# Rounded products in the input and value projections of block 2

## What is computed

```
n1 = _rmsnorm(h, norm1_w)
proj = n1 @ w_in
q, k, v, fg, u = jnp.split(proj, [512, 1024, 1536, 1544], axis=-1)
q, k = rmsnorm of q and k by head;  cum_logf = cumsum(log_sigmoid(fg + b_fgate))
a_out = softmax(q k^T / 8 + cum_logf[t] - cum_logf[s], causal) v
p_out = (trailing means of u, minus u) @ w_pool * pool_scale
h = h + concat(a_out, p_out) @ w_out
h = h + (silu(n2 @ w_gate) * (n2 @ w_up)) @ w_down
```

## Time and profile before

| | |
|---|---|
| median of 3 runs | 2333.66 us (2331.21 to 2335.54) |
| profiled execution | 2334.32 us, span 2332.6 us |
| TensorE matmul busy | 1959.3 us, 84% |
| VectorE busy | 1395.7 us, 60% |
| ScalarE busy | 1074.3 us, 46% |
| GpSimd busy | 582.4 us, 25% |
| mean granted TensorE clock | 0.905 |

### The profile page before, as it was taken

One profiled execution on the slowest core, in us unless ns is written; L12 is line 12 of the kernel. 1 busy time (PEld: TensorE's weight loads), 2 busy tenths in 40 slices (PEclk: granted clock), 3 DMA queues, 4 the chain that ended last, 5 costly groups with the idle time before them and its releaser, 6 DMA issues.

```text
span 2332.6 us, 41079 instructions
## 1 busy us (share of the span) xinstructions
PE 1959.3 (84%) x16124; PEld 1344.2 (58%) x16124; DVE 1395.7 (60%) x3264; ACT 1074.3 (46%) x2533; POOL 582.4 (25%) x541
## 2 busy tenths in 40 slices
PE   5888897988888779877855988889888885999999
PEld 4767785655545546545522623356665553667887
DVE  6654678686776676656577576666555533123554
ACT  3334545455555652224344758634454213343443
POOL 0000003332223343334344234433333330000000
PEclk8999998998888889998966996689999997999999
DMA  9932449998889999999999999999999994313555
GB/s 343 340 123 73 162 136 386 390 385 340 322 326 409 402 418 418 417 419 418 417 418 414 410 396 402 382 418 417 418 417 418 418 418 173 137 46 127 183 180 169
DMA packets 140497, 758.52 MB, mean 325 GB/s; under 512 B 16224, under 2 KB 22496, under 8 KB 74384
## 3 DMA queue, kind: packets, MB, share of 16 engines
q0 software_dynamic: 74784, 543.30, 57.1%
q1 hardware_dynamic: 60864, 208.23, 24.0%
q10 hardware_dynamic: 4656, 4.36, 0.6%
HBM read 751.60 MB, written 4.23 MB: 324 GB/s over the span
## 4 chain that ended last, share of the span: by engine, by line
PE 44%; DMA 30%; ACT 10%; DVE 10%; issue 4%; POOL 2%; ACTq 0%; SPq 0%; DVEq 0%
DMA arena<-experts,eidx 27%; PE psum L1324 7%; PE psum L842 4%; DVE arena L2475 4%; PE psum L843 4%; PE psum L844 4%; PE psum L1172 4%; DMA ring<-w_stream 2%; POOL arena L2452 2%; PE psum L1448 2%; PE psum L1621 2%; PE psum L1498 2%; DVE ring_low L2495 2%; ACT arena L2096 1%; PE psum L1197 1%
## 5 line engine op out<-in xcount | busy, mean ns | idle before, releaser
L2475 DVE CUSTOM_DVE_ANT_0 arena<-arena 128x1024 f32<-128x1024 f32 (+3 forms) x592 | 691.6, 1182 | 398.5 <-DMA arena<-experts,eidx 372.1
L2452 POOL DMA_INDIRECT arena<-experts,eidx x512 | 573.6, 1120 | 1203.8 <-PE psum L1324 925.6
L1324 PE MATMUL psum<-arena,sq 32*32 32x512 f32 x8192 | 372.2, 710 | 278.4 <-ACT sq L2104 265.6
L2090 ACT ACTIVATE arena<-arena 128x2 f32<-128x2 f32 x256 | 51.8, 202 | 585.5 <-DVE arena L2475 582.7
L1324 PEld LDWEIGHTS psum<-arena,sq 32*32 32x32 f32 x8192 | 84.4, 110 | 402.7 <-ACT sq L2104 351.0
L1172 PE MATMUL psum<-arena,ring 128*128 128x256 f32 x976 | 235.5, 396 | 4.1 <-ACT arena L1945 4.1
L1172 PEld LDWEIGHTS psum<-arena,ring 128*128 128x128 f32 x976 | 187.3, 197 | 77.1 <-issue 47.3
L1643 PE MATMUL psum<-arena,ring 128*128 128x256 f32 x704 | 162.6, 386 | 0.7 <-DVE arena L2472 0.7
L842 PE MATMUL psum<-hn_high,w_high 128*128 128x256 f32 (+1 forms) x416 | 127.8, 307 | 39.6 <-DVE ring_low L2495 21.7
L1643 PEld LDWEIGHTS psum<-arena,ring 128*128 128x128 f32 x704 | 131.2, 191 | 48.6 <-issue 31.0
L2104 ACT ACTIVATE sq<-sq,arena 128x32 f32<-128x32 f32 x512 | 136.6, 314 | 23.8
(11 more groups left out here) (377 smaller groups left out, 3380.6 us busy)
## 6 DMA issues: line engine op xcount, KB each, us to landing
ring<-w_stream SPq DMA_DIRECT2D x340, 512.0 KB
arena<-w_ada SPq DMA_DIRECT2D x48, 512.0 KB, 7.2
arena<-experts,eidx POOLq DMA_INDIRECT x512
arena<-cum_rows POOLq DMA_DIRECT2D x1, 2112.0 KB, 10.2
x<-xT SPq DMA_DIRECT2D x2, 1024.0 KB, 8.5
arena<-rel_rows ACTq DMA_DIRECT2D x4, 512.0 KB, 12.7
arena<-rel_rows POOLq DMA_DIRECT2D x1, 1024.0 KB, 10.7
k_early<-arena POOLq DMA_DIRECT2D x2, 512.0 KB, 6.3
```

The costliest lines, as they stand in the source:

```text
L1324: last = mm(bank(4 + 2 * odd + a)[QUART * b:QUART * b + QUART, :], diag[k, s, :], rows[k, s, D + a * 512:D + (a + 1) * 512], start=c == 0, ...
L2090: steps(op(pre[:, s:s + 2], pre[:, s:s + 2], ACT.Gelu))
L2452: nc.gpsimd.indirect_dma_start(rows[:, s, :], None, experts, bass.IndirectOffsetOnAxis(ap=eidx[:, n // P % 2, n % P:n % P + 1], axis=0)).t ...
L2475: return V.tensor_tensor_reduce(out=out, in0=a, in1=b, scale=1.0, scalar=0.0 if op1 == ALU.add else -TAKEN, op0=op0, op1=op1, accum_out=accum)
```

## The change

Input products 0 to 11 and the value rows of the last half take the three rounded products in place of the float32 form. The normed rows are split as in the second norm (`rounded_rows(0)` on ScalarE, `rest_row` on VectorE, between the scalings). The 16 weight tiles are split by `split_high` (ScalarE) and `split_low` (VectorE): tiles 0 to 3 on ScalarE behind the last sum of the gathers, on VectorE around the last additions and behind the norm; tiles 4 to 10 between the operations ahead of round 0; tiles 11 to 15 in rounds 0, 1, 3, 4 and 6, right behind `take_in` on ScalarE and one round later between `row_top` and `row_share` on VectorE. The forget gates and the pool products stay in float32. The counts that the feed-forward part waits for move up by 16 tiles and 8 rows.

```diff
+SPLITS = 16
 # TensorE
                 def in_product(r, ks):
-                    w = stationary(B_IN + LAST_ORDER.index(IN_ORDER[1][r]))
+                    w = tuple(a.rearrange("p (k m) -> p k m", m=P)
+                              for a in split_weights(LAST_ORDER.index(IN_ORDER[1][r])))
...
-                            pe.wait_ge(nt_ready.sem, nt_ready.ready(2 * g * KT + k))
-                        last = mm(bank(b, wide), w[:, k, :], n_t[:, k, 0:wide], start=k == 0, stop=k == KT - 1)
+                            pe.wait_ge(n_split.sem, n_split.ready(k))
+                        last = product(bank(b, wide), part(w, ALL, k), (n_high[:, k, :], n_low[:, k, :]),
+                                       k == 0, k == KT - 1)
...
-                            last = mm(bank(bank_of(g, "v", c)), n_t[:, 2 * t + k, meta + c * P:meta + (c + 1) * P],
-                                      w[:, k, :], start=t + k == 0, stop=t + k == 4)
+                            last = product(bank(bank_of(g, "v", c)),
+                                           part((n_high, n_low), ALL, 2 * t + k, slice(c * P, (c + 1) * P)),
+                                           part(w, ALL, k), t + k == 0, t + k == 4)
 # ScalarE
+            def split_high(i):
+                n = FIRST_BLOCK + BLOCK + i
+                act.wait_ge(ring_ready[n % SLOTS], 16 * (n // SLOTS + 1))
+                act.wait_ge(tile_done.sem, tile_done.ready(n - SLOTS))
+                op(last_high[:, n % SLOTS, :], ring[:, n % SLOTS, :], ACT.Copy).then_inc(w_rounded.sem, 1)
...
                     yield from ticks.until(T_IN)
+                    rounded_rows(0)
                     take_in(0)
+                    split_high(4)
                     take_in(1)
+                    split_high(5)
                     forget_logs()
                     root_of(0)
+                    split_high(6)
                     root_of(1)
+                    split_high(7)
                     take_values(0)
                     take_values(1)
+                    split_high(8)
+                    split_high(9)
                     take_in(2)
+                    split_high(10)
...
                             if LAST_DENSE.index((r, 1)) // 2 == u:
                                 take_in(r)
+                                if r + 8 < SPLITS:
+                                    split_high(r + 8)
...
             sum_out(TT - 1)
+            act.wait_ge(chosen.sem, chosen.ready(HEADS - 1))
+            for i in range(SLOTS):
+                split_high(i)
 # VectorE
+            def split_low(i):
+                s = (FIRST_BLOCK + BLOCK + i) % SLOTS
+                dve.wait_ge(w_rounded.sem, w_rounded.ready(STREAM + i))
+                V.tensor_tensor(ring_low[:, s, :], ring[:, s, :], last_high[:, s, :].bitcast(f32), ALU.subtract)\
+                    .then_inc(w_split.sem, 1)
...
                     scaled(k, n_t[:, k, 0:wide], x[:, k, cols], N1).then_inc(nt_ready.sem, 1)
+                    if g and k >= 2:
+                        rest_row(k - 2)
+                if g:
+                    rest_row(KT - 2)
+                    rest_row(KT - 1)
+                    split_low(3)
...
+                    split_low(4)
                     forget_sums()
+                    split_low(5)
                     cumulate()
                     scale_in(0)
+                    split_low(6)
                     scale_in(1)
+                    for i in range(7, 11):
+                        split_low(i)
                     for u in range(17):
                         if u < 16:
                             row_top(u)
+                        for r in range(3, SPLITS - 8):
+                            if LAST_DENSE.index((r, 1)) // 2 == u - 1:
+                                split_low(r + 8)
+                        if u < 16:
                             row_share(u)
...
+            split_low(0)
+            split_low(1)
             add_tile(TT - 1, range(4))
+            split_low(2)
             add_tile(TT - 1, range(4, KT))
```

## The result

The changed kernel takes 2352.18 us (median of 6 runs, 2345.08 to 2357.89) against 2331.49 us for the kernel before (6 runs beside it). The ratio is 1.0081, with a 95% interval of 1.006 to 1.0101: it is slower by some 19 us. I had forecast slower by 8 us, with a range of 2335 to 2348. The sign was right. The forecast change was less than half of the measured one, and the measured time lies above the range.

What follows compares the result with a forecast made beforehand. It took the tail as only half bound by TensorE, with a ScalarE-VectorE chain late in the first nine rounds; start and first softmax +2.9, rounds 0 to 8 +3.9, later rounds -1.0, clock +2.2: +8.0, about 2341.7 us, range 2335 to 2348.

Steps and rivals of the forecast that it cites:

- the later rounds: Attention rounds without splits: seven half products 0.3 us shorter each, counting only in odd rounds; 1.0 us saved.
- What the products save: TensorE in the tail: 0.6 us per input tile, 0.7 per value tile, 9.9 us less work, the most to win.
- The start: First input products wait for row splits: product 0 ends at 1984.8, product 1 at 1987.65, 1.6 us late.
- The first softmax: Splits 7 to 10 stand ahead of the first exponent: first row maximum at 2012.1, 2.9 us late.
- The rounds with splits: Rounds 0, 1, 3, 4, 6: split work and waits for landing tiles lengthen the chain; rounds 0 to 8 +3.9 us.
- The half microsecond a round on VectorE: In rounds after a split, VectorE's subtraction between row maximum and reciprocal makes it some 0.45 us late.
- The clock: TensorE idle about five times between 2007 and 2057 brings some two more falls to the lower clock; +2.2 us.
- That the splits hide: Rival: DMA waits and splits fit into ScalarE's idle half; 6.6 us less, 2327 us; chance 8%.
- The rival beyond 2346: Four clock falls on the path, or the cumulated rows' load held up beyond 2012 by ring tiles; +12 us; 20%.
- three signs of being wrong: First row maximum before 2010, rounds staying at 5.2 us, or the first product waiting for a tile, not the rests.

Runs made afterwards that it cites:

- small load: The changed kernel, but the load of the cumulated forget rows brings only head 0 (264 KB, not 2.1 MB); tail 389.5 us, ratio to before 1.005.
- the fillers: The changed kernel with 18 unused float32 products added on TensorE between the scores of round 0 and product 3; tail 393.2 us, ratio to before 1.0109.

## Why the prediction had the sign and not the size

Counted from the last sum, the first maximum came 7.8 us late (I had 2.9), rounds 0 to 8 took 13.6 us more (I had 3.9), and what follows took 3.1 us less (I had 1.0, for the later rounds alone). Before rounding that is 18.4 us, the growth of the tail. My 2.2 us for the clock belong to no one part.

**What the products save.** Right. The passes run as read from the first half; from maximum 9 to maximum 15 the rounds save 1.6 us where I took 1.0, and with no splits of tiles 4 to 15 maximum 15 comes 2.9 us earlier than before, the late load included.

**The start.** The mechanism was right: the first product starts at 1980.30, 1.76 us after the first scaling, as in the second norm. The size was short by one thing: while TensorE waited for the rests the clock went down (0.57 from 1979 to 1987), and product 1 ended near 1989.1, not 1987.65. That moved the forget gates by 1.5 us. The load of the cumulated rows came 2.7 us later than I had put it (2001.58 and not 1998.9); the other 1.2 us are the wait for the sums to reach memory first, 4.08 us where it was 2.87.

**The first softmax: the first step that failed.** I had the queue right, down to which splits stand ahead of which exponent, and summed their work. I named the load of the cumulated rows, and only asked when it would land for the maximum. I did not ask what its 2.1 MB do to a tile on the same DMA engines. Tile 9 was asked for when the last value tile ended, near 2004.4, and could be split at 2012.99, 8.6 us later. I had put no wait on it, and with the 3.3 us of a stretch without such a load it would have had none. Predicted 2012.1, measured 2017.1. Without the traffic it is 3.9 us earlier (small load).

**The rounds with splits: the second step, and the larger.** The mechanism was named (the tile that takes the slot of the product just copied, the wait for its landing, the copy and the root behind it), and the term was mis-sized. I had put 0.3, 0.6, 1.5 and 0.2 us on rounds 0, 3, 4 and 6, since I had ScalarE come late to its copy of the product by my own schedule. It came at once: on the chip ScalarE stood waiting for the end of product 3, and copied products 5 and 6 as they ended, so the whole landing less the copy falls behind it, 2.47, 2.56 and 2.50 us, and 1.69 us in round 6. That is 9.2 us and not 2.6, 6.6 us more. It does not hang on the first step, since the small load leaves these waits as they are, nor on the slow product 3, since with the fillers the wait of round 0 is 2.80 us. Rounds 0 to 8 lost 13.6 us; I had 3.9, and 2.2 for the clock, so this one term is most of the 7.5 us that were missing there, if all of the wait is on the path. Moving these five splits behind the root gives back 14.6 us of the tail, more than the waits themselves. The rest is what the passes save, which counts again once the chain doesn't wait, and the clock; the two were not told apart. The half microsecond a round on VectorE was about right (2.4 to 3.1 us in all against 2.3).

**The clock.** More falls came, as expected: the mean granted clock from 2000 to 2050 went from 0.97 to 0.80. Its share of the 18.4 us was not separated, as the filler cost what it gave.

**The rivals.** That the splits hide was wrong for this order. It is nearly true for a better one, where the splits of tiles 4 to 15 cost about 1 us. The rival beyond 2346, to which I had given 20%, came true in its number and only in part by its reasons. It named repeated falls of the clock, which came, at a cost that stays open. It also named the load held up by the ring's tiles; what happened in the changed kernel was the other way round, a tile of the ring held up by the load. The term that cost most, the landing in full behind each copy, is not in it. None of my three signs of being wrong came up either; none of them stood for a larger loss.

## What to carry to other kernels

An engine that is half idle can take more work only at a place in its queue where it would have waited anyway. Work on data that another engine's finish has only just asked for is the worst thing to put ahead of a chain: price it at the full time to landing, and not at what a schedule by hand leaves of it, and put it behind everything that the chain needs in that round. When a step moves a large transfer, ask also which small transfers now share its time.

## What the runs showed of the chip that I had not expected

In the rounds of the changed kernel a ring tile of 512 KB was ready 3.1 to 3.3 us after it was asked for, and one took 8.6 us when a load of 2.1 MB from another queue had been started 2.8 us before it. Which tile comes late changes between profiles: with the splits behind the root it was tile 8, asked for half a microsecond after the load and ready after 10.4 us. A wait of TensorE of 2.8 us ahead of the first product came with the clock at the lower level, 1.2 GHz, for most of what followed (0.57 from 1979 to 1987), as did the wait of 6 us ahead of product 3 (0.50 from 2011 to 2020); filling the second kept the clock at 2.4 GHz (1.00). The Trainium skill (TensorE: Matmul & The Clock Gate, section HAM oscillation) says that gaps bring the lower clock; the rows agree.
